# A two-layer diffusion trunk on one core: layer 1's modulation products in two bf16 passes, their low halves made by GpSimd

## The reference, cut to what matters

```python
silu_c = jax.nn.silu(c)                 # (1, 1024)
silu_cc = jax.nn.silu(c_ctx)            # (1024,)
m_l = split(silu_c @ ada_w[layer] + ada_b[layer], 6)    # ada_w[layer]: 1024 x 6144, f32
m_c = split(silu_cc @ ada_w[layer] + ada_b[layer], 6)
h_l = rmsnorm(x, norm_mix_g[layer]) * (1 + m_l[1]) + m_l[0]
...
x = x + m_l[2] * mixed
h2 = rmsnorm(x, norm_ffn_g[layer]) * (1 + m_l[4]) + m_l[3]
x = x + m_l[5] * channel_mixer(h2, ...)
```

## Time and profile before

| what | value |
|---|---|
| median of the runs (3) | 1804.65 us (1803.03 to 1805.19) |
| the profiled execution | 1803.83 us |
| its span, first to last instruction | 1802.0 us |
| mean granted TensorE clock | 0.996 |
| busy: TensorE / VectorE / ScalarE / GpSimd | 1724.5 / 1213.4 / 368.7 / 103.8 us |
| TensorE, pieces of both layers (L457), busy sum | 49.4 us in 384 records |
| transfers, whole span | 408.76 MB, mean 227 GB/s |

### The profile page before, as it was taken

How to read it: one execution, slowest core, us unless ns; L and a number is a source line. 1 busy time by engine, 2 the same in 40 slices (tenths; PEclk the granted TensorE clock), 3 DMA queues, 4 the chain that set the end, 5 groups by cost and what they waited for, 6 DMA issues and landing times.

```text
span 1802.0 us, 34744 instructions
## 1 busy us (share of the span) xinstructions
PE 1724.5 (96%) x15321; PEld 1087.4 (60%) x15321; DVE 1213.4 (67%) x1403; ACT 368.7 (20%) x671; POOL 103.8 (6%) x76
## 2 busy tenths in 40 slices
PE   6999999899999999999989888999999999999998
PEld 2434557565544444445455554969697877878695
DVE  0444476985332324115576787999999999999998
ACT  1101353343322222112115333110101000001000
POOL 0034000020000000000440010000000000000000
PEclk9999999999999999999999999999999999999999
DMA  9832201013456444231220107899999999999994
GB/s 374 320 140 70 94 1 47 1 48 141 187 187 220 181 160 170 88 94 47 94 81 37 47 24 280 354 415 418 405 418 415 418 414 419 412 415 411 414 415 197
DMA packets 98845, 408.76 MB, mean 227 GB/s; under 512 B 14008, under 2 KB 20856, under 8 KB 84368
## 3 DMA queue, kind: packets, MB, share of 16 engines
q1 hardware_dynamic: 96504, 405.54, 57.3%
q10 hardware_dynamic: 2200, 1.08, 0.2%
HBM read 405.55 MB, written 1.05 MB: 226 GB/s over the span
## 4 chain that ended last, share of the span: by engine, by line
PE 79%; DVE 11%; issue 3%; DMA 3%; ACT 2%; PEld 1%; ACTq 0%; PEldq 0%; SPq 0%; POOL 0%; DVEq 0%; POOLq 0%
PE PS L1613 12%; PE PS L1988 10%; PE PS L762 9%; PE PS L1571 6%; PE PS L1962 6%; PE PS L1964 6%; PE PS L1965 6%; PE PS L766 5%; PE PS L1477 2%; PE PS L457 2%; DVE ARENA L2084 2%; DVE ARENA L971 2%; PE PS L1339 2%; DVE ARENA L968 1%; PE PS L1950 1%
## 5 line engine op out<-in xcount | busy, mean ns | idle before, releaser
L2084 DVE TENSOR_TENSOR ARENA<-ARENA 128x2816 bf16<-128x2816 f32 (+2 forms) x184 | 567.4, 3123 | 22.9 <-DMA ARENA<-in_moe_w 22.3
L1962 PE MATMUL PS<-ARENA 128*128 128x96 bf16 x2816 | 378.5, 209 | 4.5 <-DVE ARENA L2037 1.6
L1965 PE MATMUL PS<-ARENA 128*128 128x96 bf16 x2816 | 378.3, 206 | 2.4 <-issue 2.4
L1964 PE MATMUL PS<-ARENA 128*128 128x96 bf16 x2816 | 378.3, 209 | 1.1 <-issue 1.0
L1964 PEld LDWEIGHTS PS<-ARENA 128*128 128x128 bf16 x2816 | 354.8, 126 | 9.0 <-issue 8.9
L1962 PEld LDWEIGHTS PS<-ARENA 128*128 128x128 bf16 x2816 | 346.3, 123 | 11.3 <-issue 9.1
L1965 PEld LDWEIGHTS PS<-ARENA 128*128 128x128 bf16 x2816 | 298.4, 106 | 2.8 <-issue 2.6
L1988 PE MATMUL PS<-ARENA 128*96 128x512 bf16 x960 | 216.0, 384 | 0.4 <-DVE ARENA L2084 0.4
L1613 PE MATMUL PS<-ARENA 128*128 128x512 bf16 x984 | 215.6, 379 | 0.0
L762 PE MATMUL PS<-ARENA 128*128 128x512 bf16 (+1 forms) x960 | 192.8, 354 | 8.3 <-DVE ARENA L726 8.3
L1988 PEld LDWEIGHTS PS<-ARENA 128*96 128x96 bf16 x960 | 116.2, 122 | 93.4 <-issue 0.7
(11 more groups left out here) (244 smaller groups left out, 1747.6 us busy)
## 6 DMA issues: line engine op xcount, KB each, us to landing
ARENA<-in_moe_w SPq DMA_DIRECT2D x128, 1408.0 KB, 12.9
ARENA<-in_moe_w SPq DMA_DIRECT2D x48, 1536.0 KB, 15.7
ARENA<-in_ada_w SPq DMA_DIRECT2D x24, 2048.0 KB, 10.1
ARENA<-in_ffn_w SPq DMA_DIRECT2D x15, 2048.0 KB, 7.9
ARENA<-in_w_in SPq DMA_DIRECT2D x11, 2048.0 KB, 8.2
ARENA<-in_moe_w SPq DMA_DIRECT2D x16, 1024.0 KB, 15.6
ARENA<-in_w_in SPq DMA_DIRECT2D x6, 1024.0 KB, 7.6
ARENA<-in_w_out SPq DMA_DIRECT2D x8, 512.0 KB, 4.4
```

The costliest lines, as they stand in the source:

```text
L1962: pe.matmul(out, hi[:, h][:, f], HEH[:, k, :], start=k == 0 and b % 4 == 0, stop=False, skip_group_check=True)
L1964: pe.matmul(out, hi[:, h][:, f], HEL[:, k, :], start=False, stop=False, skip_group_check=True)
L1965: mm = pe.matmul(out, lo[:, h][:, f], HEH[:, k, :], start=False, stop=k == KC - 1, skip_group_check=True)
L2084: dve.tensor_tensor(WLO[q % NSLOT][:, 0:n], RAW[q % NSLOT][:, 0:n], WHI[q % NSLOT][:, 0:n], ALU.subtract).then_inc(S("m_lo"), 1)
```

## The change

Layer 1's pieces are no longer used as f32. GpSimd splits each piece in place into word halves, in two subtractions of 128x2048 (`pool_ada_halve`), right behind its last norm step. `SC` gets a bf16 companion `SCP`: columns 0 and 1 hold the high halves of the two silu vectors, 2 and 3 the low halves. `pe_ada_mm` multiplies `SCP` with the high and then with the low half of the piece: 16 bf16 products instead of 8 f32 ones, the column groups as before. The sums for the low halves of silu stand in two more PSUM rows of each group; the selectors add them up. Layer 0's pieces stay f32.

The pieces now go to `R1` and to a new place `Z` (the first 16 KB of the arena, free after layer 0's output projection) by turns, and pieces 0 and 1 are loaded one after the other at the start, piece j later when piece j - 2 has been used. VectorE makes `SCP` once, at the start of layer 0. The four counters `h{d}{p}_qp` are folded into `h{d}{p}_upd`, which starts one higher.

```diff
         for g in range(4):
-            sel[32 * g + r, r] = 1
-            sel8[32 * g + r, 2 * g + r] = 1
+            sel[[32 * g + r, 32 * g + 2 + r], r] = 1
+            sel8[[32 * g + r, 32 * g + 2 + r], 2 * g + r] = 1
...
+        SCP = BYTES[:, 1024:1536].bitcast(BF16).rearrange("p (k c) -> p k c", c=32)
...
-                  "E2": A(24, KC, 512),
+                  "E2": A(24, KC, 512), "Z": A(0, KC, 512),
...
-        free = {6: ("norm_tp", KC)}
+        free = {6: ("norm_tp", KC), 8: ("out_mm", 2 * NT)}
...
-        FFN_LOADS += [(0 if j == 0 else 40 * j // 12, 1, ("ada", 1, j)) for j in range(12)]
+        FFN_LOADS += [(0 if j < 2 else 40 * (j - 1) // 12, 1, ("ada", 1, j)) for j in range(12)]
...
-                    place = {"w1": "R0", "w3": "R0", "ada": "R1", "w2": f"R{n % 2}"}[key[0]]
+                    place = {"w1": "R0", "w3": "R0", "ada": ("R1", "Z")[n % 2], "w2": f"R{n % 2}"}[key[0]]
...
+        def ada_halves(v):
+            v = v.rearrange("p k n -> p (k n)").bitcast(BF16).rearrange("p (k n two) -> p k n two", n=2048, two=2)
+            return v[:, :, :, 1], v[:, :, :, 0]
+
+        def pool_ada_halve(pool, j):
+            raw = raw_full(pool, ("ada", 1, j))
+            hi, lo = ada_halves(raw)
+            for n in range(2):
+                pool.tensor_tensor(lo[:, n, :], ada_view(raw)[:, n, :], hi[:, n, :], ALU.subtract).then_inc(S("ada_halved"), 1)
+
+        def dve_silu_parts(dve):
+            dve.wait_ge(S("sc_ready"), 1)
+            dve.wait_ge(S("filled"), 3)
+            dve.tensor_copy(SCP[:, :, 0:2], SC[:, :, 0:2]).then_inc(S("filled"), 1)
+            dve.wait_ge(S("filled"), 4)
+            dve.tensor_tensor(SCP[:, :, 2:4], SC[:, :, 0:2], SCP[:, :, 0:2], ALU.subtract).then_inc(S("filled"), 1)
...
-            w = ada_view(raw_full(pe, ("ada", L, j)))
             ps = B(ADA_ACC)
+            if L == 0:
+                parts_of, c = [ada_view(raw_full(pe, ("ada", L, j)))], SC
+            else:
+                pe.wait_ge(S("filled"), 5)
+                pe.wait_ge(S("ada_halved"), 2 * j + 2)
+                parts_of, c = ada_halves(items["ada", L, j]["raw"]), SCP
...
             for n in range(2):
-                for g in range(4):
-                    mm = pe.matmul(ps[32 * g:32 * g + 32, :], SC[:, 2 * kk + n, :], w[:, n, 512 * g:512 * g + 512],
-                                   start=kk == 0 and n == 0, stop=kk == 3 and n == 1)
+                for w in parts_of:
+                    for g in range(4):
+                        mm = pe.matmul(ps[32 * g:32 * g + 32, :], c[:, 2 * kk + n, :], w[:, n, 512 * g:512 * g + 512],
+                                       start=kk == 0 and n == 0 and w is parts_of[0],
+                                       stop=kk == 3 and n == 1 and w is parts_of[-1])
...
-                rows = slice(32 * g, 32 * g + 2)
+                rows = slice(32 * g, 32 * g + 4)
...
-                              ALU.mult).then_inc(S(f"h{d}{p}_qp"), 1)
+                              ALU.mult).then_inc(S(f"h{d}{p}_upd"), 1)
...
-            eng.wait_ge(S(n + "qp"), since(L, n + "qp") + 1)
-            if n_level:
-                eng.wait_ge(S(n + "upd"), since(L, n + "upd") + 3 * n_level)
+            eng.wait_ge(S(n + "upd"), since(L, n + "upd") + 1 + 3 * n_level)
...
             dve_norm_first(dve, L)
+            if L == 0:
+                dve_silu_parts(dve)
             dve_proj_first(dve, L)
...
+            dve.memset(SCP[:, :, :], 0.0).then_inc(S("filled"), 1)
...
                     pool_norm_half(pool, 1, 1)
+                    for j in range(12):
+                        pool_ada_halve(pool, j)
```

More of the change, by code:

```diff
@@ L243, in trunk @@
             for d in range(2):
-                in_layer0.update({f"h{d}{p}_qp": 1, f"h{d}{p}_upd": 3 * len(LEVELS)})
+                in_layer0.update({f"h{d}{p}_upd": 1 + 3 * len(LEVELS)})
         for step in ("s", "mx", "nb", "exp", "r", "ratio", "p", "pt", "at", "pv", "o"):
@@ L255, in trunk @@
         RAW_AT = {"R0": A(129, KC, 512), "R1": A(145, KC, 512), "E0": A(40, KC, 512), "E1": A(64, KC, 512),
-                  "E2": A(24, KC, 512),
+                  "E2": A(24, KC, 512), "Z": A(0, KC, 512),
                   "H0": A(129, KC // 2, 512), "H1": A(137, KC // 2, 512)}
-        BLOCKS = {"R0": (0, 1), "R1": (2, 3), "E0": (4,), "E1": (5,), "E2": (6,), "H0": (0,), "H1": (1,)}
-        free = {6: ("norm_tp", KC)}
+        BLOCKS = {"R0": (0, 1), "R1": (2, 3), "E0": (4,), "E1": (5,), "E2": (6,), "Z": (8,), "H0": (0,), "H1": (1,)}
+        free = {6: ("norm_tp", KC), 8: ("out_mm", 2 * NT)}
         loads = {place: 0 for place in RAW_AT}
@@ L990, in act_cross_keys @@
                 if n_level:
-                    act.wait_ge(S(f"h{d}{p}_upd"), since(L, f"h{d}{p}_upd") + 3 * n_level)
+                    act.wait_ge(S(f"h{d}{p}_upd"), since(L, f"h{d}{p}_upd") + 1 + 3 * n_level)
                 def halves(v):
@@ L1008, in pe_levels @@
                             n = f"h{d}{p}_"
[L1009 to L1012, removed]
+                            pe.wait_ge(S(n + "upd"), since(L, n + "upd") + 1 + 3 * n_level)
                         pe.wait_ge(S(f"h{p}_keys"), since(L, f"h{p}_keys") + 2 * n_level + 2)
@@ L1110, in pe_states @@
                 for d in range(2):
-                    pe.wait_ge(S(f"h{d}{p}_upd"), since(L, f"h{d}{p}_upd") + 3 * len(LEVELS))
+                    pe.wait_ge(S(f"h{d}{p}_upd"), since(L, f"h{d}{p}_upd") + 1 + 3 * len(LEVELS))
             for i in range(3):
```

## The result

Twelve runs of the changed kernel have a median of 1807.96 us (1806.58 to 1811.91), twelve of the kernel before 1803.13 us (1802.41 to 1805.19). The ratio is 1.0025, 95% interval 1.0017 to 1.0033: slower, by 4.8 us. The forecast was 1811. The profiled span grew from 1802.0 to 1807.2 us.

What follows compares the result with a forecast made beforehand. TensorE was taken to bound the kernel, with 79% of the span. From the profiled 1803.8 us, -10.4 (products) + 15.5 (hold) + 1.5 (clock) = +6.6 gave 1810.4, and 0.8 for the median gave 1811 us; range 1794 to 1818.

Steps and rivals of the forecast that it cites:

- The mechanism: GpSimd's halvings hold VectorE's low-half subtractions, and TensorE with them, in layer 0's feed-forward part: 1806 to 1818 us, chance 0.56.
- The hold: VectorE's second eight subtractions pass one per halving, 4.63 us a turn, four turns; TensorE held 15.5 us, about 2 to 22.
- the clock: TensorE's clock falls to half rate in the hold, about 3 us of it: 1.5 us added, bounds 0 and 4.
- the products: TensorE's twelve layer 1 modulation pieces take 0.98 us each in bf16 instead of 1.85: 10.4 us saved in all.
- that rival: The column groups don't overlap in bf16: 3.48 us a piece, 19.5 us lost, 1841 us in all; chance 0.05.
- Halving: Each of GpSimd's two 128x2048 subtractions a piece takes 4.45 us, at 2.1 ns an element; bounds 1.8 and 6.1 us.
- one wait, then all pass: Rival: VectorE's eight subtractions go through together in the first gap, held 2.6 us: 1797 us, faster; chance 0.17.
- VectorE isn't held: Rival: VectorE's two-tensor subtractions run as before beside GpSimd's halvings: 1799 us, or 1794 if neither waits; chance 0.15.
- Steady state: From piece 2 on, 31 us of load, halvings and blocking fit into two intervals of 37 us: no wait, 0 us.
- GpSimd is the bound: Rival: halvings over 7 us outlast a piece's two intervals, hold past 25 us: 1820 us or more; chance 0.07.
- The rest: 48 waits fewer (gain at most 3.8 us), fill and split silu (at most 1.3 us), four selector rows: 0 us.

Runs made afterwards that it cites:

- e1: The changed kernel without GpSimd's halving, the second pass multiplying the high halves by columns of zeros: 1794.18 us, ratio 0.9944 to the kernel before.
- e8: The changed kernel with pieces 0 and 1 loaded earlier, piece 0 halved right behind the norm, piece 1 after VectorE's low halves: 1795.03 us, ratio 0.9948 to before.
- e6: The changed kernel with TensorE kept busy by 14 unused products ahead of each of three waits in the hold: 1804.9 us, ratio 1.0005 to the kernel before.
- e5: The changed kernel with VectorE making the low half of the second 256 tokens in one subtraction instead of eight: 1800.29 us, ratio 0.9981 to the kernel before.
- e3: The changed kernel with GpSimd's halvings in eight times as many instructions, 128x256 each: 1796.95 us, ratio 0.9961 to the kernel before.
- e4: The changed kernel with all halvings, but TensorE making the f32 products of before: 1817.2 us, ratio 1.0074 to the kernel before.
- e7: The changed kernel with GpSimd waiting for all sixteen low halves before halving, and every piece one chunk later: 1800.67 us, ratio 0.9983 to the kernel before.
- e2: The changed kernel with GpSimd waiting for all sixteen low halves before its first halving: 1800.92 us, ratio 0.9986 to the kernel before.

## Why the prediction was right, step by step

The mechanism and its side were right. The hold was forecast 3.9 us too large; the clock (0.9), the products (0.4), the start (0.2) and the end (0.9) erred the other way and made up for 2.4 of it. That the sum came out nearer than its largest term is luck.

- *Products.* Forecast 0.98 us a piece and 10.4 us in all; measured 1.02 to 1.03 us and 10.0 (246.86 less 236.87; 9.9 in e1). The column groups do overlap in bf16, so that rival is out. The overhead around the four rounds was 0.15 us, not the 0.11 carried over from f32.
- *Halving.* Forecast 4.45 us. Two in a row alone take 7.16 us (e8), so 3.58 us. This was the term most off: 1.75 ns an element, where the earlier trace rows gave 2.1. (The fill behind its lower bound reads no tensor, so it was not near in kind.) The group's mean of 4485 ns seems to confirm the forecast, but blocked halvings are in it, as the spread of the same group in the changed kernel shows (shortest, median and longest in ns; first and last start): from 3.60 through 3.65 to 7.8 us. A group's mean is no price where instructions hold each other.

```profile
L457 POOL TENSOR_TENSOR ARENA<-ARENA x24: 3598/3650/7785, 449.2 to 670.1; 128x2048 bf16<-128x2048 f32 x24
```

- *The hold.* Forecast 4.63 us a turn and 15.5 us of TensorE; measured 3.74 us a turn, by the shorter halving alone. The second eight end at 465.64 instead of 453.81, 11.8 us later, 0.2 of it from a later start; the other 11.6 us reach TensorE in full, as e6's 11.4 do there. The number of turns (four), the passing of one instruction per turn, and the last four at once are as forecast. E5 and e3 bear out that turns are per instruction; "one wait, then all pass" would have given e3 no pace of 0.75 us, and "VectorE isn't held" falls with the first row of the hold.
- *The clock.* Forecast 1.5 us, bounds 0 to 4; measured 2.4 (e6). The fall was seen in the earlier trace rows, but the return took 6 us of dense work here, against 3 there and 3 in e4's profiled execution. From one row of before its length could not be had; what sets it is open.
- *Steady state.* Forecast 0, and 0 it is: e4's stage is that of before to 0.01 us, and in all runs whose head leaves the clock at 1.00 or restores it before the first piece the bf16 stage is 236.9 us. The 0 rests on cover, though: the prediction counted that of the chunk that needs L390's result, and e7 shows another, that of the copy L528 queued behind L390, which one chunk's shift took away (2.1 us of waiting, and the clock behind it). "GpSimd is the bound" is out as well: it waits 124 us for loads.
- *The rest* (48 waits, silu parts, selector rows). Forecast 0. TensorE reaches the transposes 0.24 us later, inside the up to 1.8 us by which other runs differ there; e1, which holds these parts too, is 0.17 us earlier. They are not told apart from nothing.

The sum, with what was measured: -10.0 + 14.0 (11.6 of waiting and 2.4 of clock) + 0.2 + 0.9 after the stage, in place of -10.4 + 15.5 + 1.5. The 0.9 us after 711 us was not forecast. It arises in the expert part, whose first product is 4.3 us later than before and whose last 5.2 (L1962 from 1126.7 to 1762.0, here L1986 from 1131.0 to 1767.2). E2, e4 and e5 have the same instructions there and show none of it, other runs up to 0.5 us and e6 -0.8 (e7 apart), so it is not shown to come from the change. Of the 3.0 us between the forecast of 1811 and the measured 1808, 1.5 us are the starting point: the forecast set out from the 1804.65 us of three runs, and twelve runs of before have 1803.13.

By the port rule of the Trainium skill (SBUF — State Buffer, "SBUF: two separate sides") the engine that starts first has the shared pair for its whole instruction. The traces agree: four L660 were each held by a halving (3.74 us apart instead of 0.34), and in e2 a halving was held by L390 (until 463.4). What set the price here is who comes next, and the runs show that too: at the end of an instruction the waiting engine has its turn even if the other has more queued. So many short VectorE instructions against several long GpSimd ones in a row are the dear case.

## What to carry to other kernels

Work for GpSimd is not hidden just because GpSimd is idle: look at which VectorE instructions it overlaps, and whether TensorE follows them without slack. Here the price was one GpSimd instruction per VectorE instruction as long as GpSimd had any queued: four turns of 3.74 us for eight subtractions, as four halvings stood in the queue. So make GpSimd's instructions short there (e3), or load and halve the first piece ahead of the race (e8); the same work went from 4.8 us slower to 7 or 8 us faster by that. And count a hold of TensorE twice, once for the wait and once for the clock after it.

## What was not expected of the hardware

- VectorE's L653, which reads PSUM, was not held: in e8 the four take 1.90 us from 448.31 on, in the midst of GpSimd's 445.30 to 452.46, as in runs without a halving there. In the earlier trace rows the same operation on SBUF operands was held.
- A subtraction of 128x2048 f32 less bf16 to bf16, in place, takes GpSimd 3.58 us; the same in eight instructions comes to 4.9 us by the shortest of e3 (607 ns) and to 6.4 on the mean, blocked time included (153.3 us over 24).
- TensorE's clock fell in e3 although it never waited more than 0.36 us at a time; in 452 to 456 us, where the granted clock was 0.81 in the mean, it had short pauses between pairs of products.
